# Second expert round's rows read by GpSimd's queue, the next tile's rows added ahead of the norm, biases masked head by head

## What is computed

```python
for i in range(2):
    ...
    y = conv_mixers(h, ...) if i == 0 else attn_mixers(h, ...)
    x = x + g1 * y
    h = modulate(rmsnorm_2(x, norm_g[i, 1]), sh2, sc2)
    x = x + g2 * hier_moe(h, ...)          # 2 of 32 experts a token, each (silu(h wg) * (h wu)) wd
return rmsnorm_2(x, final_norm_g)

# attn_mixers, the topk attention: 8 heads, 512 queries, 512 keys
logit_c = q_c . k_sel * scale + bias_c[rel_bucket(dist_c)]      # only the 128 best-scored keys count
p_c = softmax(logit_c);  out_c = p_c . v_sel
# the differential attention: 4 heads with two softmax maps each, one bias a head
attn = softmax(q1 . k1 * scale + b_d) - lam * softmax(q2 . k2 * scale + b_d)
```

## Time and profile before

| | |
|---|---|
| median of 3 runs | 4026.84 us (4025.64 to 4028.89) |
| the profiled execution's own time | 4019.26 us |
| its span | 4017.5 us |
| TensorE matmul busy | 86% |
| VectorE busy | 42% |
| ScalarE busy | 17% |
| GpSimd busy | 5% |
| mean granted TensorE clock | 0.934 |
| expert stage, layer 0 (weights asked for to last store) | 2310 to 2880 us |
| expert stage, layer 1 | 3428 to 3978 us |
| residual stage, layers 0 and 1 | 2885 to 2923 us, 3984 to 4017 us |
| topk attention | 3199 to 3277 us |

### The profile page before, as it was taken

The page is one execution under the profiler, slowest core; times in us unless marked ns, Lnnn a source line. Parts: engine busy times, 40 slices in busy tenths (PEclk is TensorE's granted clock), DMA queues, the critical chain, the costliest instruction groups (busy, mean ns, idle before and its releaser), DMA issues. The chain is left out here.

```text
span 4017.5 us, 38010 instructions
## 1 busy us (share of the span) xinstructions
PE 3464.8 (86%) x13936; PEld 1747.1 (43%) x13937; DVE 1689.9 (42%) x3091; ACT 701.4 (17%) x1412; POOL 195.2 (5%) x261
## 2 busy tenths in 40 slices
PE   8998999888899999889889967778689888688775
PEld 4454434885445444378634532223243344323221
DVE  3235556775232555666638410000238685200002
ACT  1132214000112330310010100000122253100001
POOL 0001010001000001000000000000000040000000
PEclk9998999999999999899889979999889999799897
DMA  3115452004121236200243099999533331899996
GB/s 106 67 48 213 137 171 58 1 1 144 51 84 32 68 94 197 54 11 1 78 155 122 0 391 427 428 428 399 204 105 113 108 85 59 339 428 419 428 428 249
DMA packets 208086, 696.40 MB, mean 173 GB/s; under 512 B 22248, under 2 KB 105704, under 8 KB 182608
## 3 DMA queue, kind: packets, MB, share of 16 engines
q1 hardware_dynamic: 178864, 590.60, 38.4%
q0 software_dynamic: 29088, 104.00, 7.1%
HBM read 636.28 MB, written 58.28 MB: 173 GB/s over the span
## 5 line engine op out<-in xcount | busy, mean ns | idle before, releaser
L345 PE MATMUL bank<-fm,w 128*128 128x512 f32 (+1 forms) x912 | 398.0, 597 | 11.5 <-DMA w<-in_ab_w_in 6.5
L2796 PE MATMUL bank<-experts_wu,experts_hs 128*64 128x512 f32 x1120 | 265.3, 629 | 73.1 <-DMA experts_wu<-in_moe_w_up 73.1
L345 PE MATMUL bank<-w,fm 128*128 128x512 f32 (+2 forms) x768 | 315.0, 566 | 6.4 <-DMA w<-in_w_in 6.4
L2796 PE MATMUL bank<-experts_wg,experts_hs 128*64 128x512 f32 x1120 | 271.9, 641 | 54.6 <-DMA experts_wg<-in_moe_w_gate 40.3
L2796 PE MATMUL bank<-experts_wd,fm 128*64 128x512 f32 x1120 | 265.8, 630 | 54.1 <-issue 37.9
L2861 DVE TENSOR_TENSOR fm<-bank,fm 128x512 f32<-128x512 f32 x35 | 37.0, 1056 | 636.6 <-PE bank L2796 636.6
L345 PEld LDWEIGHTS bank<-fm,w 128*128 128x128 f32 (+1 forms) x912 | 172.5, 190 | 234.7 <-issue 221.3
L728 PE MATMUL bank<-fm,side_w 128*128 128x512 f32 x512 | 249.3, 612 | 6.8 <-DMA side_w<-in_w_in 5.4
L345 PEld LDWEIGHTS bank<-w,fm 128*128 128x128 f32 x768 | 141.7, 194 | 179.1 <-issue 153.8
L2796 PEld LDWEIGHTS bank<-experts_wu,experts_hs 128*64 128x64 f32 x1120 | 83.9, 144 | 252.6 <-issue 157.5
L2796 PEld LDWEIGHTS bank<-experts_wg,experts_hs 128*64 128x64 f32 x1120 | 94.2, 148 | 228.2 <-issue 225.0
(11 more groups left out here) (483 smaller groups left out, 4898.8 us busy)
## 6 DMA issues: line engine op xcount, KB each, us to landing
experts_wg<-in_moe_w_gate SPq DMA_DIRECT2D x64, 2048.0 KB, 19.5
experts_wu<-in_moe_w_up SPq DMA_DIRECT2D x64, 2048.0 KB
experts_wd<-in_moe_w_down SPq DMA_DIRECT2D x64, 2048.0 KB
ada_w<-in_ada_w POOLq DMA_DIRECT2D x96, 512.0 KB, 4.9
w<-in_w_in SPq DMA_DIRECT2D x40, 512.0 KB, 3.9
fm<-expert_rows SPq DMA_DIRECT2D x35, 512.0 KB, 21.6
expert_rows<-fm POOLq DMA_DIRECT2D x35, 512.0 KB, 10.1
w<-in_w_in SPq DMA_DIRECT2D x16, 1024.0 KB, 7.2
```

What stands on the lines that cost most here:

```text
L345: ins = pe.matmul(bank, lhsT, rhs, start=(n == 0), stop=(n == len(todo) - 1))
L2796: ins = pe.matmul(bank[rows, :], lhs[:, k, rows], weights[:, s, k, cols], start=(k == 0), stop=(k == chunks - 1))
```

## The change

Three edits. In the expert stage, the read of round 1's rows goes from SP's order to GpSimd's, right behind its wait for the scatters, with a count of its own (`second_rows`); SP neither waits for the scatters nor reads these rows. In the residual stage, VectorE adds tile t + 1's rows before it asks for tile t's mean. In the attentions with biases, every head's loads have a count of their own, GpSimd waits for one head's four loads and counts each head masked, and VectorE waits for its own head's.

```diff
-            loaded = [st.count(f"bias{i}_loaded") for i in range(ring)]
+            loaded = [[st.count(f"bias{i}_{a}_loaded") for a in range(n_bias)] for i in range(ring)]
...
-                                         ).then_inc(*loaded[g % ring].inc(16))
+                                         ).then_inc(*loaded[g % ring][a].inc(16))
...
                 for g in range(units):
-                    pool.wait_ge(*loaded[g % ring].at(16 * loads * (g // ring + 1)))
                     for a in range(n_bias):
+                        pool.wait_ge(*loaded[g % ring][a].at(16 * TILES * (g // ring + 1)))
                         b = bias_sb[g % ring][:, a, :, :]
-                        ins = pool.tensor_tensor(b, b, masks[:, 2 * (g % 2):2 * (g % 2) + 2, :], ALU.add)
-                    ins.then_inc(*masked.inc())
+                        pool.tensor_tensor(b, b, masks[:, 2 * (g % 2):2 * (g % 2) + 2, :], ALU.add).then_inc(*masked.inc())
...
-                    dve.wait_ge(*masked.at(s // 4 + 1))
+                    dve.wait_ge(*masked.at(s // 4 * n_bias + (a if mix is None else 0) + 1))
...
-        sp.wait_ge(*rows_written)
-        load_rows(1)
         load("moe_w_down", wd, down_done, down_loaded, 1, seats)
         sp.wait_ge(*gathered.at(1))
         load_rows(2)
...
         pool.wait_ge(*rows_written)
+        pool.dma_start(xs[:, :], rows[P:2 * P, :]).then_inc(*second_rows.inc(16))
         with pool.Fori(0, rounds_of(pool)) as p:
...
-            pe.wait_ge(*rows_loaded.at(16 * q))
+            if isinstance(q, int):
+                pe.wait_ge(*second_rows.at(second_rows.total))
+            else:
+                pe.wait_ge(*rows_loaded.at(16 * q - 16))
...
+                add_rows(dve, 0)
                 for t in range(TILES):
-                    add_rows(dve, t)
+                    if t + 1 < TILES:
+                        add_rows(dve, t + 1)
                     norm.ask(dve, t)
                     finish(t)
```

More of the change, by code:

```diff
@@ L663, in attention @@
             bias_sb = [st.sb(f"bias{i}", [P, n_bias, 2, SEQ]) for i in range(ring)]
-            loaded = [st.count(f"bias{i}_loaded") for i in range(ring)]
+            loaded = [[st.count(f"bias{i}_{a}_loaded") for a in range(n_bias)] for i in range(ring)]
             masked = st.count("bias_masked")
-            loads = TILES * n_bias
             @st.block.sync
@@ L2726, in item_experts @@
     yready, yfree, yread = one("y_ready"), one("y_free"), one("y_read")
-    ystored = chip.new_count()
+    ystored, second_rows = chip.new_count(), chip.second_rows
     def rounds_of(eng):
@@ L3181, in program @@
         chip.rows_fetched = [chip.new_count() for _ in range(2 * TILES)]
-        chip.rows_spread = chip.new_count()
+        chip.rows_spread, chip.second_rows = chip.new_count(), chip.new_count()
         chip.expert_rows = nc.dram_tensor("expert_rows", [ITEMS * SLOTS, D], F32, kind="Internal").ap()
```

## The result

The changed kernel took 4006.96 us (median of 5 runs, 3997.59 to 4009.78) beside 4026.84 us (4025.64 to 4034.88), ratio 0.9938 with the 95% interval [0.9925, 0.9951]. (The two medians by themselves give 0.9951, 19.9 us, which lies within 1.1 us of the forecast; the text goes by the ratio and its interval.) The profiled execution took 4009.78 us and was the slowest of the five.

What follows compares the result with a forecast made beforehand. Expert stages were taken as bound by DMA at 428 GB/s with one hole per layer, residual stages as VectorE and ScalarE chains. 5.5 + 0.7 + 10.8 + 1.8 = 18.8 us off 4026.84 gives 4008.0 us; range 4002 to 4016.

Steps and rivals of the forecast that it cites:

- Rows, layer 0: Expert stage: round 1's rows on GpSimd's queue land near 2364, before TensorE needs them; gain 5.5 us (5.1 to 5.9).
- under 3: Sign in layer 0's expert stage: TensorE's transposes of round 1 come near 2366 with a wait under 3 us.
- The hole: Empty DMA stretch in layer 0's expert stage, 2385 to 2392, share 0.27; forecast to close, with a share near 1.
- Rows, layer 1: Expert stage: TensorE gets round 1's rows 0.6 us earlier, wait and hole much as before; gain 0.7 us (-1 to +2).
- the rows were held by the scatters and not by the queue: Layer 1's expert stage: SP issues the rows at 3483.70, right when the scatters have landed; they arrive 9.8 us later.
- both holes close: Rival, expert stages: layer 1's rows too arrive well ahead, up to 5.4 us sooner; 4004 us; chance 0.10.
- SP no longer stands at the wait with the down weights behind it [...] worth nothing: Layer 1's expert stage: down weights could go 2.5 us earlier, but the engines are full then, so no gain.
- slower, by late rows: Rival, expert stages: weight loads starve the rows' read on GpSimd's queue; landing at 22.4 us cancels all gains; chance 0.02.
- Adds ahead of the norm: Residual stages: next tile's adds cover ScalarE's squares; gain 5.2 us in layer 0, 5.6 in layer 1, together 10.8.
- tile 1: Residual stages: VectorE waits for tile 1's second fetch, losing 0.3 to 0.9 us in layer 0, 0.1 to 0.4 in layer 1.
- Biases head by head: Topk attention: GpSimd's mask burst starts 1.8 us earlier and the stage gains that; bounds -0.7 and +4.3.
- The step ahead of it: Topk attention: GpSimd's first mask waits for four quarter loads instead of eight, so it begins 1.8 us earlier.

Runs made afterwards that it cites:

- the changed kernel's last run: The changed kernel, measured again beside the kernel before with the adds ahead of the norm alone; ratio 0.9996 to before, which took 4028.73 us.
- before again: The kernel before, unchanged, run to have its own profile on the third chip; before stood at 4025.97 us there.
- the first four runs: Kernel before with rows' move alone (0.9972), adds' order alone (0.9971), biases head by head alone (1.0009); changed kernel without the biases edit (0.9942); before at 4027.16 us.

## Why the prediction was right or wrong

**Rows, layer 0 (forecast 5.5).** In the first profile right in mechanism and near in size, 6.7 (4.7 in the kernel with the rows alone). The rows landed at 2369.4 (2359.03 + 10.4), half a microsecond past the late end of the forecast's 2358 to 2369, because the scatters had landed only at 2359.0 (2354 taken); TensorE waited 3.8 us against "under 3". The hole closed and no other opened. In executions with late scatters the term is nothing (575.4 us) or a loss of 6 to 7 us (581.8 to 582.6).

**Rows, layer 1 (forecast 0.7). This is the step that failed.** The prediction held that "the rows were held by the scatters and not by the queue", from one profile in which SP passed the wait at 3483.70. Measured: 7.6 us, and the rival "both holes close", given 0.10, is what the first result shows. In that one stage the scatters were late; in others of the same kernel they are not. The prediction read how that execution went as how the kernel goes. The term of 0.7 us is right only for a stage like the one it was read from: where the gate loads began at 36.9 us in layer 1, the changed order gave 557.1 us against 556.7. Had it compared layer 0 (gate loads at 39.4 us into the stage, scatters landed by 48.4) with layer 1 (37.1 and 56.2) it could have seen the switch.

Here is the switch, from 28 stages of 14 profiles: all kernels in which neither SP's gate loads are held nor the scatters moved nor the down weights put off. Times are in us, from the stage's first weight load; for the rows read by SP "landed" is the time at which SP asked for them, by which the scatters were in.

```
rows read by   stages  gate loads   landed      wait for rows  layer 0        layer 1
SP, early         5    38.7 - 39.5  48.0 - 50.1   9.0 - 11.2   575.2 - 575.6  555.1 - 555.8
SP, late          5    35.4 - 37.1  56.2 - 62.2  11.1 - 14.0   574.5 - 575.4  555.0 - 556.7
GpSimd, early     7    38.6 - 39.5  46.7 - 49.8   1.5 -  3.8   568.9 - 570.8  549.1 - 549.9
GpSimd, late      4    36.8 - 37.5  56.1 - 57.3  13.2 - 14.6   575.4 - 578.9  557.1
GpSimd, later     7    34.0 - 35.7  61.5 - 67.9  18.8 - 24.3   581.8 - 582.6  562.5 - 563.8
```

Nothing lies between 37.5 and 38.6. The DMA view of five microseconds says why (packets, MB, share of 16 engines; q1 is SP's queue, q0 GpSimd's). First the first profile after, layer 1, 3467 to 3472 (35 to 40 us into the stage; gate loads asked for only at 3471.19), then layer 1 of the changed kernel's last run, 3478 to 3483 (40 to 45 us), with gate loads begun at 3471.57:

```profile
q0 software_dynamic: 568, 2.07, 101.4%
q1 hardware_dynamic: 3, 0.02, 0.8%
```
```profile
q1 hardware_dynamic: 123, 1.75, 81.9%
q0 software_dynamic: 120, 0.43, 21.2%
```

Between SP's round 0 loads and its gate loads of round 1 there is a gap in which the scatters have the engines to themselves and move 2.07 MB in 5 us; beside SP's loads they move 0.43. In the second window the two queues got as many packets, 123 and 120, but SP's held some 14 KB each and GpSimd's some 3.6; hence the share in bytes. If the gate loads begin 1 to 5 us sooner, what is left of the scatters crawls. Then the rows are asked for late; with gate loads at 36.8 to 37.5 us the changed order gains nothing, and with gate loads before 36 us it is worse than the old one. The timelines of that same run, layer 1:

```profile
3464.25 7.09 PE L2796 MATMUL bank<-experts_wg,experts_hs 128*64 128x512 f32 x32 [3.56 <-issue]
...
3471.57 2.53 SPq L2744 DMA_DIRECT2D experts_wg<-in_moe_w_gate  x2
...
3487.99 1.85 SPq L2744 DMA_DIRECT2D experts_wd<-in_moe_w_down  x2
...
3505.54 0.57 POOL L2768 DMA_DIRECT2D fm<-expert_rows  x1 [40.51 <-DMA expert_rows<-normed,experts_row_of]
...
3512.04 1.97 PE L2788 MATMUL bank<-consts,fm 128*128 128x128 f32 x8 [24.28 <-DMA fm<-expert_rows]
```

And its windows there:

```profile
3495.00:3502.00 7.00, 0.00 (x0) 0.00 (x0) 0.00 (x0) 0.00 (x0) 0.00 (x0) 0.50 1.00 428
3502.00:3509.00 7.00, 0.00 (x0) 0.00 (x0) 0.00 (x0) 0.00 (x0) 1.13 (x2) 0.50 0.98 418
3509.00:3526.00 17.00, 12.72 (x48) 4.93 (x50) 0.00 (x0) 1.68 (x3) 0.00 (x0) 0.67 0.23 87
```

SP issues the down weights at 3487.99, long before the scatters are in, because nothing holds it any more. The engines run on at full rate (428 GB/s while TensorE stands), and then the stream is empty for 17 x 0.77 = 13 us. On the same chip, SP's and TensorE's timelines of the kernel with the adds alone, layer 1:

```profile
3496.92 0.34 SPq L2738 DMA_DIRECT2D fm<-expert_rows  x1
3498.22 1.85 SPq L2746 DMA_DIRECT2D experts_wd<-in_moe_w_down  x2
...
3500.43 1.97 PE L2788 MATMUL bank<-consts,fm 128*128 128x128 f32 x8 [11.48 <-DMA fm<-expert_rows]
```

The rows take 3.5 us, and the stage has its 555.0 us. Layer 0 of the same two runs tells what the removed wait did, for there the gate loads began at 35.4 us in both. First the kernel with the adds alone (SP and TensorE), then the changed kernel (GpSimd and TensorE):

```profile
2375.18 0.35 SPq L2738 DMA_DIRECT2D fm<-expert_rows  x1
...
2378.58 1.97 PE L2788 MATMUL bank<-consts,fm 128*128 128x128 f32 x8 [13.97 <-DMA fm<-expert_rows]
```
```profile
2373.26 0.57 POOL L2768 DMA_DIRECT2D fm<-expert_rows  x1 [34.02 <-DMA expert_rows<-normed,experts_row_of]
...
2383.88 1.97 PE L2788 MATMUL bank<-consts,fm 128*128 128x128 f32 x8 [18.80 <-DMA fm<-expert_rows]
```

The scatters landed at like times, 62.2 and 61.5 us into the stage: the down weights did not delay them. But the rows then took 3.4 us in the old order, on engines that had run out of loads, and 10.6 in the new one, beside the down weights. TensorE got them 6.5 us later in the stage, and the stage was 6.4 us longer (581.8 against 575.4). In the four other stages with gate loads at 35.5 to 35.7 us it is the same: landed at 61.7 to 63.3, rows 10.2 to 11.2 us later. In the two stages with gate loads at 34.0 us the scatters themselves were later, at 66.4 and 67.9, and the rows took 7.8 and 6.5; the old order was never seen with loads at 34.0, so how much of that is due to the down weights is open.

So the sentence "SP no longer stands at the wait with the down weights behind it [...] worth nothing" failed too: where the scatters are late, that wait keeps the down weights out of the rows' way, and without it 6 to 8 us a layer are lost. This is the last rival, "slower, by late rows", in kind: a read beside weight loads. Its sum missed it, for it asked for a landing time of over 22 us, and the rows never took over 11.2 until TensorE's turn; what it compared them with was 9.8 us, and in such stages of the old order it is 3.4. The price is what on two chips cancels the rest. That the down weights' place does it, and not GpSimd's queue as such, is read from these traces. No kernel was run in which GpSimd reads the rows and SP still waits for the scatters ahead of the down weights alone.

Windows of layer 1 with SP held for six scatters: 6 us at a DMA share of 0.60 at the handover, and after that no hole. Then, held for two, 31 us of layer 0 and 45 us of layer 1, the stretches in which the others have the hole:

```profile
3464.00:3470.00 6.00, 4.19 (x20) 1.47 (x17) 1.03 (x1) 0.60 (x1) 0.57 (x1) 0.89 0.60 207
3470.00:3520.00 50.00, 39.03 (x158) 14.12 (x156) 3.60 (x5) 3.26 (x6) 0.89 (x2) 0.84 1.00 424
```
```profile
2364.00:2395.00 31.00, 27.12 (x118) 9.34 (x118) 2.33 (x3) 3.26 (x6) 0.00 (x0) 0.89 1.01 428
3475.00:3520.00 45.00, 36.12 (x160) 12.68 (x156) 3.61 (x5) 3.85 (x7) 1.10 (x2) 0.92 1.01 428
```

The Trainium skill ("DMA: Bandwidth & Descriptors", section "Issuing engines are not separate DMA queues") says that the transfers of all issuers share 16 engines and interleave, and that another issuer saves issuing time alone. The first half agrees with the 0.43 beside 1.75 MB. The second does not: the same 512 KB took 10.4 us on the other queue against 18.3 at the end of SP's, and where the scatters were early the expert stages became 5 to 8 us shorter.

**Adds ahead of the norm (forecast 10.8).** Right, 12.1 by the first profile and 11.8 in the kernel with the adds alone. Layer 0 gave 6.0 and layer 1 6.2, against 5.2 and 5.6, a little above the upper bounds of 5.8 and 6.0. VectorE never waited at tile 1 in layer 1, where 0.1 to 0.4 us were taken off. In layer 0 it waited 0.64 us there, as forecast. The fetches issued under the adds in layer 0 took 1.43, 1.81 and 1.62 us instead of 0.94:

```profile
2883.14 1.43 POOL L2927 DMA_INDIRECT rows<-expert_rows,experts_row_of  x1 [0.30 <-issue]
2884.87 1.81 POOL L2927 DMA_INDIRECT rows<-expert_rows,experts_row_of  x1 [0.30 <-issue]
```

The Trainium skill ("SBUF — State Buffer", section "Who interferes with whom") says that a VectorE instruction with two SBUF inputs contends with a GpSimd one that reads SBUF. For these fetch issues the runs do not settle it: in layer 1 the issues under four adds took 0.94, 0.95 and 1.10 us, the sixth fetch of layer 0 took 1.84 to 1.97 us in three kernels without this edit too (rows only, biases only, before again), and 0.93 or 0.94 in 8 of the 16 profiles that have it. What stretches a fetch issue is open; the stage's length does not follow it. The residual stages were 31.8 to 32.5 and 27.0 to 27.4 us in all 16 profiles that have this edit, on every chip. Of the three edits it is the one that is worth the same in every execution.

**Biases head by head (forecast 1.8).** The step ahead of it is right: the first mask began 4.1 us after SP's first load (3187.03 to 3191.14) instead of 6.5, 2.4 us earlier. It buys nothing that can be measured, 1.0009 [0.9995, 1.0022] alone and 0.9938 with it against 0.9942 without (different chips). So the 1.8 us failed as a gain of the stage: its start moved and its end did not follow, which the prediction had named as a sign of being wrong. That the first profile's topk stage was 11 us longer need not be its work: lengths of 88 to 90 us or 78 to 82 us come with it (3 long ones in 14 profiles) and without it (1 in 6).

**The sum.** 18.8 us were forecast and 24.9 measured by the ratio. The first profile's parts are 6.7 + 7.6 + 12.1 = 26.4 us and nothing for the masks. So layer 1's rows make up most of the difference (6.9 us more than forecast); the adds and layer 0's rows were 2.5 us better and the masks 1.8 worse. An execution with two early stages gives 12 to 14 for the rows and 12 for the adds, some 4001 us. One with two late ones gives the 12 of the adds less 0 to 14. The four profiled executions of the changed kernel fit that in order: 4009.78 us with two early stages (and the long topk stage), 4006.93 with one, 4021.76 and 4029.54 with none. That its medians, 4003 to 4029 us, are mixtures of such executions is likely, and not shown by more than these four. That the first result came out early in both layers, and near the range, was luck: the forecast knew nothing of the switch.

**What stays open.** What sets the switch. SP's gate loads follow the end of TensorE's first gate product, which begins at 26.4 us into the stage in one execution and at 29.9 in another and takes 7.1 to 10.1 us. The gap ahead of it is 3.5 to 7.1 us, put down by the profile to nothing it shows, but the other timelines lead one step back: in all 28 stages the product begins 1.5 to 1.8 us after VectorE has written the counts of the rounds, for which the code has TensorE wait. That work begins with a copy of TensorE's last result. In the 12 stages on the two chips without any early stage the copy begins 0.1 us after TensorE's recorded end, in the other four late ones 1.4 to 1.9 us after it, and in the 12 early ones 2.1 to 3.5 us. What holds the copy is not shown (the profile models the ends of TensorE's products, so it may hide there). Nor is it known what favours it: of the 28 stages in the table, 7 of 8 were early on the chip of the first four runs, none of 8 on the next, 2 of 4 on the third and none of 4 on the fourth, where changed kernels and kernels with the old order alike were late. What switches the topk stage is open as well.

## What to carry to other kernels

A wait that seems to cost nothing may be keeping a large load out of the way of a small transfer on which the next round depends; before it is removed, ask what it lets through, and compare how the same place went in each layer or repetition within the profile. Where two queues race, order the race by a count (SP holds its next load until the first scatters have landed) instead of hoping for its outcome. An edit that is worth 0.6% on one chip and nothing on another is measured on several, with the kernel before profiled beside it.

## What the runs showed of the hardware

- Two loaded queues got as many packets and not as many bytes: in 5 us SP's plain loads of 2 MB moved 1.75 MB in 123 packets and GpSimd's scatters 0.43 MB in 120; alone, the scatters moved 2.07 MB in 568.
- A read of 512 KB took 18.3 us behind SP's loads, 10.4 on GpSimd's queue beside them, and 3.4 on engines that had run out of loads.
- A faster TensorE went with a slower stage, because the next loads wait for its product. In the changed kernel's last run, layer 1, round 0's gate product took 7.09 us at a granted clock of 1.00, and the stage 563 us where 549 is possible. In the first profile after, layer 0, it took 10.03 us, with a granted clock of 0.55 in the window below (the lower level is 0.50, 1.2 GHz), and the stage had its gain.

```profile
2339.00:2344.00 5.00, 5.00 (x16) 1.52 (x14) 0.00 (x0) 0.00 (x0) 0.00 (x0) 0.55 0.99 374
```

- One stage, the topk attention, has two lengths, with or without the change: 78 to 82 us at a granted clock of 0.86 to 0.92, and 88 to 90 us at 0.81 to 0.83 (0.92 with the scores issued twice).
